# Order of work on ScalarE and VectorE beside a gated linear attention: drains behind the exponentials, weight split ahead of the gate differences

## The reference

```python
px = jnp.split(hx @ w_in[l], IN_SPLIT_IDX, axis=-1)      # 512 tokens
pc = jnp.split(hc @ w_in[l], IN_SPLIT_IDX, axis=-1)      # 256 context tokens
...
def hgrn2_prep(q, i, f, lb_d):
    fg = lb_d + (1.0 - lb_d) * jax.nn.sigmoid(f)
    return silu(q) * HG_HEAD_DIM ** -0.5, 1.0 - fg, i, jnp.log(fg)     # q, k, v, logf
...
def step(S, inp):                                        # gla_chunked, one chunk
    b = jnp.cumsum(lf, axis=-2)
    diff = b[:, :, :, None, :] - b[:, :, None, :, :]
    decay = jnp.where(mask, jnp.exp(jnp.minimum(diff, 0.0)), 0.0)
    A = jnp.einsum('bhtk,bhsk,bhtsk->bhts', qc, kc, decay)
    o = jnp.einsum('bhts,bhsv->bhtv', A, vc) + jnp.einsum('bhtk,bhkv->bhtv', qc * jnp.exp(b), S)
    S_new = exp(b_last)[..., None] * S + einsum('bhsk,bhsv->bhkv', kc * exp(b_last - b), vc)
```

## Time and profile before

| What | us |
|---|---|
| median of 3 runs | 2184.19 (2182.41 to 2184.21) |
| the profiled execution, its own time | 2182.41 |
| its span, first to last instruction | 2180.8 |
| TensorE busy | 2055.3 (94% of the span) |
| VectorE busy | 1246.4 (57%) |
| ScalarE busy | 908.8 (42%) |
| GpSimd busy | 296.7 (14%) |
| TensorE in the stage of the change, 1340 to 1640 us | 270.2 of 300 |

### The profile page before, as it was taken

One profiled execution on the slowest core, in us unless ns is written; L12 is line 12 of the kernel. 1 busy time (PEld: TensorE's weight loads), 2 busy tenths in 40 slices (PEclk: granted clock), 3 DMA queues, 4 the chain that ended last, 5 costly groups with the idle time before them and its releaser, 6 DMA issues. The chain is left out here.

```text
span 2180.8 us, 26996 instructions
## 1 busy us (share of the span) xinstructions
PE 2055.3 (94%) x9546; PEld 1628.6 (75%) x9546; DVE 1246.4 (57%) x1910; ACT 908.8 (42%) x1403; POOL 296.7 (14%) x380
## 2 busy tenths in 40 slices
PE   8999889999999999999999998899877999999997
PEld 6666556888888677678888867788765677888886
DVE  3666437788677646766664443788546544333333
ACT  4333535444422434344442235566447634222222
POOL 0033411000000101000000002777410001000000
PEclk9999999999999999999999999999998999999999
DMA  5511013566445322222233211111110022322321
GB/s 171 148 47 39 1 39 102 170 193 192 154 154 163 106 86 80 86 78 96 96 96 119 93 58 58 40 40 40 59 39 1 1 87 78 96 96 96 116 94 51
DMA packets 52779, 193.93 MB, mean 89 GB/s; under 512 B 5808, under 2 KB 8528, under 8 KB 52312
## 3 DMA queue, kind: packets, MB, share of 16 engines
q1 hardware_dynamic: 44824, 165.18, 23.9%
q0 software_dynamic: 7344, 27.27, 4.0%
q10 hardware_dynamic: 528, 0.40, 0.1%
HBM read 189.15 MB, written 3.68 MB: 88 GB/s over the span
## 5 line engine op out<-in xcount | busy, mean ns | idle before, releaser
L196 PE MATMUL psum<-xH,w_hi 128*128 128x512 f32 x1800 | 727.4, 404 | 42.1 <-DVE xL L1372 21.5
L196 PE MATMUL psum<-xL,w_hi 128*128 128x512 f32 x1800 | 709.4, 394 | 0.0
L196 PE MATMUL psum<-xH,w_lo 128*128 128x512 f32 x1800 | 708.9, 394 | 0.0
L166 DVE TENSOR_TENSOR w_lo<-w_raw,w_hi 128x1024 fp32r<-128x1024 f32 (+1 forms) x273 | 354.3, 1298 | 342.5 <-ACT w_hi L160 342.1
L160 ACT ACTIVATE w_hi<-w_raw 128x1024 fp32r<-128x1024 f32 (+1 forms) x273 | 303.3, 1111 | 416.6 <-PE psum L196 407.4
L196 PEld LDWEIGHTS psum<-xH,w_hi 128*128 128x128 f32 x1800 | 342.9, 191 | 140.6 <-DVE xL L1372 36.8
L196 PEld LDWEIGHTS psum<-xH,w_lo 128*128 128x128 f32 x1800 | 342.9, 190 | 73.5
L196 PEld LDWEIGHTS psum<-xL,w_hi 128*128 128x128 f32 x1800 | 343.5, 191 | 71.5 <-issue 3.9
L196 PE MATMUL psum<-hidH,w_hi 128*128 128x512 f32 x528 | 206.2, 391 | 0.0
L196 PE MATMUL psum<-hidH,w_lo 128*128 128x512 f32 x528 | 205.4, 389 | 0.0
L196 PE MATMUL psum<-hidL,w_hi 128*128 128x512 f32 x528 | 205.4, 389 | 0.0
(11 more groups left out here) (321 smaller groups left out, 2510.9 us busy)
## 6 DMA issues: line engine op xcount, KB each, us to landing
w_raw<-in_up SPq DMA_DIRECT2D x132, 512.0 KB, 3.5
w_raw<-in_down SPq DMA_DIRECT2D x48, 704.0 KB, 4.1
mod_raw<-in_mod POOLq DMA_DIRECT2D x48, 512.0 KB, 3.9
w_raw<-in_sb_in SPq DMA_DIRECT2D x26, 512.0 KB, 3.5
w_raw<-in_ev_in SPq DMA_DIRECT2D x23, 512.0 KB, 3.7
w_raw<-in_od_in SPq DMA_DIRECT2D x20, 512.0 KB, 3.5
w_raw<-in_ev_out SPq DMA_DIRECT2D x8, 512.0 KB, 3.6
w_raw<-in_od_out SPq DMA_DIRECT2D x8, 512.0 KB, 3.5
```

The lines of the kernel that those rows point to most:

```text
L166: nc.vector.tensor_tensor(w_lo[:, s % SPLIT, 0:w.cols], raw[:, s, 0:w.cols], w_hi[:, s % SPLIT, 0:w.cols].bitcast(F32), ALU.subtract).then ...
L196: mm = nc.tensor.matmul(acc, a[:, slot % SPLIT, cut], b[:, k0 + k, :], start=start and n == 0, stop=stop and n == 2)
```

## The change

Two orders are changed, and nothing is added or removed.

On ScalarE, in slice n of `decays`, the drains `v_out` and `kd_out` stood ahead of the exponential of job n. They now stand behind it, and behind `diag_out` and `prepare`, which never fall into the same slice as a drain.

On VectorE, in iteration p, the split `w_lo` of chunk c + 2 (`self.low`) stood behind `gla(p - 11)`, so behind the differences, `states` and `select`. It now stands ahead of it.

```diff
                 def decays(n):
                     if n is None:
                         return
-                    for half in range(2):
-                        hd = due(n, 4 + half, 2 * LEVELS, HG)
-                        if hd is not None:
-                            v_out(hd, half)
-                        u = due(n, 6 + half, LEVELS, U7)
-                        if u is not None:
-                            kd_out(u, half)
                     if 0 <= n < JOBS:
                         act.wait_ge(g["diff"], n + 1)
                         d = dec[:, n % 4, :]
...
                     u = due(n, 1, LEVELS, U7)
                     if u is not None:
                         prepare(u)
+                    for half in range(2):
+                        hd = due(n, 4 + half, 2 * LEVELS, HG)
+                        if hd is not None:
+                            v_out(hd, half)
+                        u = due(n, 6 + half, LEVELS, U7)
+                        if u is not None:
+                            kd_out(u, half)
...
                 for p in range(len(PARTS)):
                     if p == 0:
                         self.low(dve, 0, 0, True)
+                    if p in ENDED and ENDED[p] + SPLIT < w.n:
+                        self.low(dve, 0, ENDED[p], True)
                     if p in (2, 3):
                         dve.wait_ge(sec_par, 64)
                         nc.vector.tensor_copy(level_mask[p - 2][:, :], masks_in[p - 2][:, :])
                     gla(job(p - AHEAD))
-                    if p in ENDED and ENDED[p] + SPLIT < w.n:
-                        self.low(dve, 0, ENDED[p], True)
                     if p in GAINS:
                         head_gain(GAINS[p])
```

## The result

The changed kernel took 2199.07 us (median of 4 runs, 2198.18 to 2199.62) against 2184.2 us for the kernel before (median of 4 runs, 2182.41 to 2184.55). The ratio is 1.007, with a 95% interval of 1.0056 to 1.0085: slower by 14.9 us. The forecast was 2197, slower. The two profiled executions differ by a little more, 16.1 us (spans of 2180.8 and 2196.9 us).

A forecast was written before the change was run, and what follows sets the result against it. TensorE, busy 94% of the span, was taken as the bound. Terms 4.2 + 3.6 + 3.3 + 5.2 - 4.7 + 2.5 = +14.1 us gave 2196.5 on 2182.4 or 2198.3 on 2184.2; forecast 2197, range 2186 to 2204.

The forecast's parts named there:

- the heads did not win: Rival: the split's gain in the heads outweighs the drains' cost, so faster, about 2177 us; chance 0.12.
- the drains were not hidden: Rival: slices between preparation and use absorb the drains, no change, 2180 to 2186 us; chance 0.12 (hidden or half).
- The start: Slices 1 to 5: +4.2 us, of which +3.3 at v_out(0, 0) with level(1) and +0.9 at v_out(0, 1).
- v_out(1, 0): Second head's drain, p = 28: split waits for w_hi, delaying differences, exponential and drain: +2.0 us.
- v_out(2, 0) and (3, 0): Same pattern at heads 2 and 3, with TensorE late from an earlier stall: +0.8 us each, bounds 0 and 2.0.
- kd_out(2, 0), (4, 0), (6, 0): Drains of units 2, 4 and 6 come after exponentials that wait for their difference: +1.1 us each.
- kd_out(3, 0), (5, 0): Chunk ends, slices 27 and 41, where both edits fall: TensorE waits +2.6 us more at each.
- kd_out(1, 0): Unit 1, slice 13, a chunk end: drain in time as TensorE runs at half clock after the 4.4 us wait.
- The heads: Parts 63, 64, 66 and 68: the split's new place shortens TensorE's waits, -4.7 us in all.
- The clock: More clock falls at the start and units 3 and 5, fewer in the heads, 1.7 us each: +2.5 us.
- The signs: Profile after: ScalarE's waits for VectorE near 76 us, v_out waits about 10, kd_out about 11, head_sin about 6.
- The rule on VectorE and GpSimd: Exclusive port lock: differences starting beside a GpSimd product wait some 0.5 us more at nine sites; left out of the sum.

The follow-up runs named there:

- e1: The kernel before with only the drains moved behind the exponentials, the weight split in its old place: 2197.26 us, ratio 1.0072.
- e11: The kernel before with only the 8 v_out moved behind the exponentials, kd_out and the split in their old places: 2191.35 us, ratio 1.0031.
- e2: The kernel before with only the weight split moved ahead of gla, the drains in their old place: 2170.49 us, ratio 0.9949.
- e6: The kernel before with all drains behind the exponentials and the split ahead of gla only from part 60 on: 2188.01 us, ratio 1.0017.
- e4: The kernel before with the split ahead of gla only before part 60, the drains in their old place: 2184.35 us, ratio 1.0013.
- e9: The changed kernel with two drains, kd_out(3, 0) and kd_out(5, 0), put back ahead of their exponential: 2187.37 us, ratio 1.001.
- e5: The kernel before with an extra ScalarE copy of about 0.5 us, waiting for nothing, ahead of each of the 24 drains: 2188.3 us, ratio 1.0015.

## Why the prediction was right

The direction, the mechanism and the total (+14.1 forecast, +14.9 measured) held. That the total is within 1 us is partly luck: single terms were off by up to 2.0 us, the start and the heads one way, v_out, unit 1 and the clock the other. The rivals fell: the heads did not win (e1 alone is +14.4, and they give back 9.4 against 24), and the drains were not hidden (eleven waits, 22.5 us). The terms one by one, as waits of the changed kernel's trace against the earlier trace rows:

- **The start.** Forecast +3.3 for v_out(0, 0) with level(1). The waits grew from 2.45 to 5.63 us, +3.2; TensorE is 2.15 us later behind it than before, as it had come 1.0 us earlier. The extra 0.9 for v_out(0, 1) did not come: TensorE ran at half clock behind the wait (granted 0.50 from 1372 to 1378 us), and by then the drain was in time. The bound of that term should have let the fall hide it, as the forecast did for unit 1.
- **v_out(1, 0).** Forecast +2.0, measured 1.76. **v_out(2, 0) and (3, 0).** Forecast 0.8 each, measured 1.58 each. The step that halved them, because TensorE comes late from the stall of the unit before, was wrong. These two wait 0.66 us in e1, where that stall is there, and 0.68 and 0.67 in e11, where it is not: the stall changes nothing. The split's place adds the other 0.9 us. The upper bound, 2.0, held.
- **kd_out(2, 0), (4, 0), (6, 0).** Forecast 1.1 each, measured 0.82, 0.82 and 1.11. e1 has the same three numbers, so this term is the drains' alone.
- **kd_out(3, 0), (5, 0).** Forecast +2.6 each, measured +2.65 and +2.68. e1 splits it: 1.4 from going behind the exponential, 1.3 from the split and its wait for `w_hi` inside the chain.
- **kd_out(1, 0).** Forecast 0, measured 1.08. It was costed as covered by the half clock behind the gates' 4.58 us wait; the cover was not long enough. In e1, with the split behind `gla`, there is no wait here.
- **The heads.** Forecast -4.7, measured -6.7 (14.6 to 7.9 us). The two long waits for head_sin were 3.57 and 3.58 us and became 1.90 and 1.59 (two short ones), so they fell by 1.7 and 2.0, not by 1.2 and 1.1 (0.15 of the second is for head_sin, 1.44 for kd_out(7, 0)). The 4.06 us wait fell to 2.11 instead of 2.9. The 1.90 us wait of part 68 became 0.77, as forecast. e2 shows the same 2.11 and 1.90 with the drains in their old place, so it is the split's edit alone. The first three fell by more than the split's length, because the instruction behind it got shorter too, as the rows below show.

The timelines of VectorE from the select to head_sin, at part 64 before (its select and split are in the earlier trace rows) and then in the changed kernel:

```profile
1571.27 0.94 DVE L2407 TENSOR_SCALAR sb_hT<-sb_hT,cols 128x512 f32<-128x512 f32 x1
1572.13 0.68 DVE L2414 TENSOR_TENSOR head_sin<-psum,rope 128x512 f32<-128x512 f32 x1
```

```profile
1591.38 0.72 DVE L2384 COPY_PREDICATED gla_weights<-gla_masks,psum 128x512 f32<-128x512 uint8 x1 [3.14 <-PE psum L2518]
1592.00 0.50 DVE L2407 TENSOR_SCALAR sb_hT<-sb_hT,cols 128x512 f32<-128x512 f32 x1
1592.42 0.68 DVE L2414 TENSOR_TENSOR head_sin<-psum,rope 128x512 f32<-128x512 f32 x1
```

From the start of the select to that of head_sin it was 2.70 us and is 1.04 us: 1.22 less for the split and 0.44 for `head_gain` (0.94 us long before, 0.50 now). That is the 1.67 us by which the wait fell. At the next site the same sum is 2.93 against 1.00 us.

- **The clock.** Forecast +2.5, worked from 1.7 us for a fall. A fall at units 3 and 5 cost 2.5 and 2.8 us; at the start, 60.42 us from one wait to the next against 55.83 before, less 3.3 of waits between them, leaves 1.3; the heads had one fall instead of three, and of their 9.4 us the 6.7 of waits leave -2.7. Together +3.9.

The terms measured are +3.2 at the start, +4.9 for v_out(1 to 3, 0), +2.8 and +5.3 for kd_out of the even and of the odd units, +1.1 for unit 1, some +0.5 for the gates' longer wait, -6.7 for the heads and +3.9 for the clock: +15.0. TensorE is behind by 14.5 us at the last head mean, 15.5 counted from its arrival in the stage, so 0.5 us are in no term. The fall behind the heads, 1.6 us, is outside this sum.

**The signs.** Most of those that the forecast named came: the drains' waits (9.2 us in 4 places, 13.3 in 7), the clock of 0.50 at the start and at units 3 and 5, and VectorE's longer wait for `w_hi`. One failed: ScalarE's waits for VectorE did not stay near 76 us but are 107.4. The drains' 10.8 us of work, and 8.3 us of waiting for TensorE's transposes ahead of them, used to pass while a difference was under way; the waiting is 0.1 us now, and ScalarE stands idle ahead of the exponential instead. That this is the cause of the rise is argued from these numbers. The sum did not use the sign.

**The part that the sum did not show.** The forecast's terms add the two edits per place, and at units 3 and 5 and at v_out(1, 0) it did see that they meet. It did not say that without that meeting the split's edit is a gain of 12.4 us (e2) and the drains a loss of 14.4 (e1). e6, e4 and e9 place the interaction: ahead of part 60 the split's move costs 1.5 us as long as the drains stand ahead of the exponential, and 11 us when they stand behind it. Of this, 7.0 us are waits in the changed kernel's trace and the rest mostly clock.

**The rule on VectorE and GpSimd.** In the timeline of the second head above, the split at 1426.01 takes 1.44 us where the one of the earlier trace rows took 1.23: GpSimd's product of 1.02 us had begun at 1425.35 and ended at 1426.37. The product behind it, which began 0.31 us after the split, took 1.71 us where one of its form took 0.73 at 1421.96 in the trace before. The mean of the 22 splits of the stage goes from 1253 to 1374 ns, and that of the second halves of the differences falls from 810 to 691 ns, so the split now meets products that the differences met before. The Trainium skill (SBUF — State Buffer, Who interferes with whom) has the port pair of the two engines as an exclusive lock, held by the first. The trace agrees within 0.15 us here: 1.23 behind 1426.37 would end at 1427.60, and the split ended at 1427.45. Its price in the chain is 0.2 us at this site, and at kd_out(2, 0) and (4, 0) nothing (0.82 us against 1.1 forecast without it), not the 0.5 at each of nine sites that the forecast had worked out from the rule.

## What to carry to other kernels

In a list that an engine works off in order, a short instruction takes over every wait that stands ahead of it. Ask what the instruction in front waits for, not how long it is: 12 us of added copies cost 3.2 us here (1.1 to 5.7), and the same drains behind a wait cost 14.4 (12.7 to 18.8). Two edits on two engines that meet in one chain (ScalarE makes `w_hi`, VectorE splits it, ScalarE waits for what follows) are not to be costed by themselves; test each alone, since one of them may be the gain that the other hides. And put the drain of a buffer that the busiest engine needs ahead of anything that waits: with four drains put earlier, two at the start and those of units 3 and 5, and the split early only in the heads, this kernel is at 2167.71 us. What each of the four brings was not measured by itself.

## What the runs showed of the hardware

The length of a wait alone does not say whether TensorE's clock falls after it. e1 has two equal waits of 2.75 us, at units 3 and 5; here are lines of its timeline, and of its stretches of 2 us behind each:

```profile
1467.09 0.30 PE L2535 MATMUL psum<-ident,gla_keys_decayed 128*128 128x128 f32 x1 [2.75 <-ACT gla_kd_tm L2191]
1523.50 0.45 PE L2535 MATMUL psum<-ident,gla_keys_decayed 128*128 128x128 f32 x1 [2.75 <-ACT gla_kd_tm L2191]
```

```profile
1468.00:1470.00 2.00, 2.00 (x10) 1.00 0.55 156
1524.00:1526.00 2.00, 2.00 (x6) 0.50 0.46 68
1526.00:1528.00 2.00, 2.00 (x8) 0.78 0.48 195
```

After the first the clock stays at 1.00, after the second it is 0.50, and the transposes take 0.30 and 0.45 us. The same is seen for shorter ones: 2.28 us before had no fall and 2.11 us in e2 had none, but the 2.11 us wait of the changed kernel had one, as its stretches show, and so had 2.01 and 1.98 us in e5:

```profile
1584.00:1586.00 2.00, 0.98 (x3) 1.00 0.00 0
1586.00:1588.00 2.00, 2.00 (x7) 0.56 0.00 0
```

The two cases overlap further than that. After a wait of 1.90 us for head_sin the clock fell in e1, e4 and e11 and stayed at 1.00 in the traces before and after and in six others. And e1 has a wait of 3.56 us without a fall, the stretch behind it at full clock, and one of 1.90 us with a fall, 28 us later:

```profile
1588.00:1590.00 2.00, 2.00 (x10) 1.00 0.10 35
1616.00:1618.00 2.00, 2.00 (x6) 0.50 0.00 0
```

All waits from 4.0 us up in the stage had a fall. The forecast took 2.28 us as safe and 3.57 us as not; in the runs falls begin at 1.90 us, and one wait of 3.56 us had none. What decides between equal waits was not found. The Trainium skill (TensorE: Matmul & The Clock Gate, HAM oscillation) describes that an idle gap throttles the array anew, and counts the slower products behind it as a cost on top of the gap. The traces agree for the waits from 4.0 us up, with 2.5 to 2.8 us on top of a 4.0 us wait.
